# The rows' two parts kept in the order of the features, and twelve gather products moved ahead of the branch

## The chip, the cores and the metric

One core of a Trainium2 chip runs the whole program. The metric is device time in microseconds, from the start to the end of one execution. The kernel before took 949.39 us (median of three runs, 949.18 to 949.49). All profile rows are of one further execution, which took 949.4 us and whose span in the trace is 947.4 us. Engines: PE is TensorE with PEld its weight loads, DVE is VectorE, ACT is ScalarE, POOL is GpSimd, SP issues most transfers.

## The reference

Two transformer blocks in float32 over 256 tokens of 1024 features. The change touches only the mixture of experts at the end of the second block:

```python
xn = rms_norm(h, ffn_norm_g)                      # (1, 256, 1024)
group_prob = softmax(xn @ w_rg + b_rg)            # 4 groups, the best one is taken
sel = expert logits of that group                 # 8 experts, the best two are taken
out = zeros_like(xn)
for e in range(32):
    hid = silu(xn @ w_gate[e]) * (xn @ w_up[e])   # 1024 -> 256
    out = out + (hid * cw[..., e:e + 1]) @ w_down[e]
h = h + out                                       # then the final rms_norm
```

## The kernel before

The program first runs all dense layers (up to about 700 us), in which every float32 product is made of three products of rounded parts (`pe_mm3`, L493 to L495). The experts follow in one of two forms, and a branch on a number in memory (`flag`, read at L2970, tested at L2977) chooses between them: when no expert has more than `CAP` = 48 tokens, the sparse form runs, else the dense form. These inputs take the sparse form.

In the sparse form the tokens of each expert are gathered by products. `SEL0` is a 0/1 matrix: for 128 tokens and for each of a set of `SET_E` = 8 experts it has 48 columns, one for each slot of the expert. The normalised rows are the stationary operand (128 tokens by 128 features), the 384 columns of `SEL0` are the moving one, and what comes out in PSUM is 128 features by 8 x 48 slots. As rounding would lose bits, the rows are kept in two parts, `XN[0]` (high, rounded, called XNH in the profile) and `XN[1]` (low, the rest, XNL), and both go through the same product. There are four sets of experts (q = 0 to 3), 8 chunks of features (k), 2 parts and 2 tiles of tokens (t): 32 products for each set, 128 in all. All are made at L2481 (`pe_gather`), except for the first twelve of set 0 (high part, k = 0 to 5, both tiles), which are made at L2569 at the start of `pe_sparse`.

Chunk k holds the features k, k + 8, k + 16 and so on, since the weights of the experts are loaded in that order. In the kernel before, the rows are put into that order when the parts are made. `by_chunks` is a view of X with chunks ahead of features: ScalarE reads X by it with a step of 8 elements (32 bytes) and writes `XN4[0]` without gaps (L1532, two instructions of 1024 elements); VectorE does the same for the low part (`low`, L2013, eight instructions of 256 elements). Each stationary operand `XN4[i][:, t, k]` is then 128 neighbouring elements.

The order around the branch is written out by hand, engine by engine:

- PE: the router's products, 9 warm-up products, three products that count ranks (L1002 to L1005, semaphore `rank_mm`), 2 warm-up products (`pe_warm`, L996; each is two instructions), the branch, the twelve products of L2569, then twenty of L2481: low part of k = 0 to 3, high part of k = 6 and 7 (their banks come free by ScalarE's evictions), low part of k = 4 to 7. Then `pe_rise` (L2507), the first expert pair.
- DVE: routing, then the largest count (`most`, L2017), the ranks (L2019), a copy of the count to an integer (`flag`, L2021), the two halves of `SEL0` (`dve_mark`, L1944, semaphore `sel`), eight low parts in the order k = 0 and 1 of both tiles, k = 2 and 3, and so on (semaphore `xn_lo`), then the combine weights.
- ACT: the high parts (L1532), two small exponentials, the branch, then the evictions of the gathered features (`act_gather`, L2623).

All five engines wait for `flag` and read it before they branch.

Of the kernel before, what the change touches and what calls it, by code (L numbers as in the profile page):

```python
# [7 lines left out]
ALU = mybir.AluOpType  # L8
ACT = mybir.ActivationFunctionType
# [155 lines left out]
def build(nc, A, out):  # L165
    with ExitStack() as ctx:
# [202 lines left out]


        ROUTER = U["router", 0, 0]

        def raw_of(i):
            kc, w = shape_of(i)
# [379 lines left out]
        def pe_main():  # L754
# [238 lines left out]
            def pe_warm(n):  # L993

                for _ in range(n):
                    PE.matmul(PB[0][:, 0:256], ident, cst("upper", 256), start=True, stop=True, skip_group_check=True)  # L996
# [7 lines left out]
                      skip_group_check=True)  # L1004
            PE.matmul(PB[1][:, 64:96], UO[:, 128:256], MK[:, 32:64], start=False, stop=True, skip_group_check=True).then_inc(S["rank_mm"], 1)  # L1005
            pe_warm(2)

# [163 lines left out]
        def act_main():  # L1173
# [355 lines left out]
                ACTE.activation(UO[:, 128 * i:128 * i + 128], cst("upper", 128, 128 * i), ACT.Copy).then_inc(S["const_r"], 1)  # L1529
            ACTE.wait_ge(*scaled("ffn"))  # L1530
            for t in range(2):
                ACTE.activation(XN4[0][:, t], by_chunks[:, t], ACT.Copy, scale=rs_of["ffn"][:, t:t + 1]).then_inc(S["xn_hi"], 1)  # L1532
            ACTE.wait_ge(S["route_e"], 1)
            ACTE.activation(eg, eg, ACT.Exp).then_inc(S["step_a"], 1)
            ACTE.wait_ge(S["route_e"], 2)
# [18 lines left out]
        def dve_then(ins):  # L1554

            steps[0] += 1
            ins.then_inc(S["step_d"], 1)

        def dve_after():
            DVE.wait_ge(S["step_d"], steps[0])  # L1560
# [356 lines left out]
        def rt(n):  # L1917
            o = rt_at[0]
            rt_at[0] += n
            return KW[:, o:o + n]  # L1920
# [4 lines left out]
        fst, snd, q_e = [v3(rt(8), 2, 4) for _ in range(3)]  # L1925
        e2 = rt(2)
        rank, cw = rt(64), rt(64)
        most, flag = rt(1), rt(1).bitcast(I32)
        wa, wb = rt(2), rt(2)

        def b3(ap, n):
# [16 lines left out]
        def dve_route():  # L1948
            L3 = v3(L, 2, 36)
            DVE.wait_ge(S["logits"], 2)  # L1950
            DVE.wait_ge(*scaled("ffn"))
            b1 = banks_of(("router", 0))[1]
            for t in range(2):
                DVE.scalar_tensor_tensor(L3[:, t], PB[b1][:, 36 * t:36 * t + 36], rs_of["ffn"][:, t:t + 1], rb, ALU.mult,
                                         ALU.add).then_inc(evicted(("router", 0))[0], 1)
            DVE.wait_ge(*evicted(("router", 0)))
            G, E = L3[:, :, 0:4], L3[:, :, 4:36].rearrange("p t (g n) -> p t g n", g=4)
            order8 = cst("order", 8, 4).unsqueeze(1).unsqueeze(1).to_broadcast([128, 2, 4, 8])

            def step(ins):  # L1960

                dve_then(ins)
                return steps[0]

            def behind(n):
                DVE.wait_ge(S["step_d"], n)

            a = step(DVE.tensor_reduce(fst, E, AXX, ALU.max))
            g = step(DVE.tensor_reduce(gm, G, AXX, ALU.max))
            behind(a)  # L1970
            a = step(DVE.tensor_tensor(v_e, E, b8(fst), ALU.is_equal))
            behind(g)
            for t in range(2):
                g = step(DVE.scalar_tensor_tensor(v_a[:, t], G[:, t], gm[:, t:t + 1], cst("order", 4), ALU.is_equal, ALU.mult))
            behind(a)
            a = step(DVE.tensor_tensor(v_e, v_e, order8, ALU.mult))
            behind(g)
            g = step(DVE.tensor_reduce(q_a, v_a, AXX, ALU.max))
            DVE.tensor_tensor(eg, G, b3(gm, 4), ALU.subtract).then_inc(S["route_e"], 1)
            behind(a)  # L1980
            a = step(DVE.tensor_reduce(q_e, v_e, AXX, ALU.max))
            behind(g)
            g = step(DVE.tensor_tensor(og, v_a, b3(q_a, 4), ALU.is_equal))
            behind(a)
            a = step(DVE.tensor_tensor(o1, v_e, b8(q_e), ALU.is_equal))
            behind(a)
            a = step(DVE.scalar_tensor_tensor(el, o1, NEG, E, ALU.mult, ALU.add))
            behind(a)
            a = step(DVE.tensor_reduce(snd, el, AXX, ALU.max))
            behind(a)  # L1990
            a = step(DVE.tensor_tensor(v_e, el, b8(snd), ALU.is_equal))
            behind(a)
            a = step(DVE.tensor_tensor(v_e, v_e, order8, ALU.mult))
            behind(a)
            a = step(DVE.tensor_reduce(q_e, v_e, AXX, ALU.max))
            behind(a)
            a = step(DVE.tensor_tensor(o2, v_e, b8(q_e), ALU.is_equal))
            behind(a)
            a = step(DVE.tensor_tensor(el, o1, o2, ALU.add))
            behind(a)  # L2000
            DVE.tensor_tensor(MK[:, :].rearrange("p (t g n) -> p t g n", t=2, g=4), el, b8(og), ALU.mult).then_inc(S["mask_d"], 1)

            a = step(DVE.tensor_tensor(snd, snd, fst, ALU.subtract))
            behind(a)
            a = step(DVE.tensor_tensor(snd, snd, og, ALU.mult))
            behind(a)
            DVE.tensor_reduce(e2, snd, AXX, ALU.add).then_inc(S["route_e"], 1)

            def low(t, r):

                DVE.wait_ge(S["xn_hi"], t + 1)
                hi, lo = [x[:, t, 2 * r:2 * r + 2] for x in XN4]
                DVE.scalar_tensor_tensor(lo, by_chunks[:, t, 2 * r:2 * r + 2], rs_of["ffn"][:, t:t + 1], hi.bitcast(F), ALU.mult,  # L2013
                                         ALU.subtract).then_inc(S["xn_lo"], 1)

            DVE.wait_ge(S["rank_mm"], 1)
            dve_then(DVE.tensor_reduce(most, PB[1][:, 64:96], AXX, ALU.max))  # L2017
            DVE.wait_ge(S["mask_d"], 1)
            DVE.scalar_tensor_tensor(rank, PB[1][:, 0:64], 1.0, MK[:, :].bitcast(F), ALU.add, ALU.mult).then_inc(S["rank"], 1)  # L2019
            dve_after()  # L2020
            DVE.tensor_copy(flag, most).then_inc(S["flag"], 1)  # L2021
            DVE.wait_ge(S["rank"], 1)
            for t in range(2):
                dve_mark(SEL0, t, 0).then_inc(S["sel"], 1)
            for r in range(4):
                for t in range(2):
                    low(t, r)
            DVE.wait_ge(S["step_a"], 1)
            dve_then(DVE.tensor_reduce(pg, eg, AXX, ALU.add))
            DVE.wait_ge(S["step_a"], 2)  # L2030
            dve_then(DVE.tensor_scalar(wa, e2, 1.0, None, ALU.add))
            dve_after()
            dve_then(DVE.reciprocal(pg, pg))
            dve_then(DVE.reciprocal(wa, wa))
            dve_after()
            dve_then(DVE.scalar_tensor_tensor(wa, wa, 0.5, pg, ALU.mult, ALU.mult))
            dve_after()
            dve_then(DVE.tensor_tensor(wb, wa, e2, ALU.mult))
            one, two = [o.rearrange("p t g n -> p t (g n)") for o in (o1, o2)]
            dve_then(DVE.tensor_tensor(one, one, b3(wa, 32), ALU.mult))  # L2040
            dve_after()
            dve_then(DVE.tensor_tensor(two, two, b3(wb, 32), ALU.mult))
            dve_after()
            dve_then(DVE.tensor_tensor(o1, o1, o2, ALU.add))
            dve_after()
            DVE.tensor_tensor(cw[:, :].rearrange("p (t g n) -> p t g n", t=2, g=4), o1, b8(og), ALU.mult).then_inc(S["weights"], 1)
# [363 lines left out]
        def sparse(late):  # L2410
# [16 lines left out]
                return p // PS + 1 if p % PS == PS - 1 and p + 1 < NP else 0  # L2427

            def gather_bank(q, k):
                return PB[(6, 7, 2, 3, 0, 1, 6, 7)[k] if q == 0 else (6, 7, 4 + (PS * q - 1) % 2)[k % 3]]  # L2430

            def rise_bank(p):
                return PB[4 + p % 2]
# [7 lines left out]
            def selected(q, t=1):  # L2441
                return S["sel"], 2 * q + t + 1
# [21 lines left out]
            def pe_gather(q, k, parts=(0, 1)):  # L2464
# [4 lines left out]
                elif q > 0 and k == 0:  # L2469
                    PE.wait_ge(*selected(q))  # L2470
                if q == 0 and 1 in parts:
                    PE.wait_ge(S["xn_lo"], 2 + 2 * (k // 2))
                if q > 0 and k < 2:
                    PE.wait_ge(S["yy_lo"], 2 * (PS * q - 3) + k + 1)
                elif q > 0 and k == 2:
# [84 lines left out]
                        m.then_inc(S["spread"], 1)  # L2560

            def pe_sparse():
                PE.wait_ge(S["evict1"], K_LAST[1])
                PE.wait_ge(S["evict0"], K_LAST[0])
                for t in range(2):
                    PE.wait_ge(*selected(0, t))
                    PE.wait_ge(S["xn_hi"], t + 1)
                    for k in range(6):
                        PE.matmul(gather_bank(0, k)[:, 0:384].rearrange("p (e n) -> p e n", e=SET_E), XN4[0][:, t, k], slots_of(SEL0, t),  # L2569
                                  start=(t == 0), stop=False, skip_group_check=True)  # L2570
                for k in range(4):
                    pe_gather(0, k, (1,))
                for k in (6, 7):
# [384 lines left out]
        normed = ExitStack()  # L2958
        XN = [sbe("XNH", 2048, R, normed), sbe("XNL", 2048, R, normed)]
        SEL0, MK, UO = [sbe(n, w, R, normed) for n, w in (("SEL0", 1024), ("MK", 64), ("UO", 256))]  # L2960
        XN4 = [x[:, :].rearrange("p (t k q) -> p t k q", t=2, k=8) for x in XN]
        by_chunks = X[:, :].rearrange("p (t q k) -> p t k q", t=2, k=8)
        sp_main()
        pe_main()
        act_main()
# [32 lines left out]
```

## Time and profile before

| | |
|---|---|
| median of three runs | 949.39 us |
| the profiled execution | 949.4 us, of which the span is 947.4 us |
| PE busy | 936.2 us, 99% of the span |
| DVE busy, ACT busy | 533.4 us, 471.5 us |
| granted TensorE clock over the span | 0.996 |
| gather products (L2569, L2481) | 12 + 116 recorded |
| first product of the gather | 710.04 us |
| first product of the first expert pair | 716.08 us |

Read it so: the engine busy times say who has no idle time; the chain of waits, followed back from the last instruction, says which engine held the end at each moment; the timeline of the few microseconds around the branch says who waits for whom there. "PEld" rows are the loads of the stationary operand, one for each product, which run beside the product before. The time between the starts of two loads in a row is their spacing; it is found from a merged row as (length of the row minus one load) divided by (count minus one).

### The profile page before, as it was taken

To read this page: it belongs to the slowest core of one execution; us is meant where nothing else is said; L and a number is where in the kernel's file an instruction comes from. 1 tells how busy PE (TensorE), PEld (TensorE's weight loads), DVE (VectorE), ACT (ScalarE), POOL (GpSimd) and SP (SyncE) were. 2 spreads that over 40 slices of the span, in tenths; PEclk is the share of its full clock that TensorE was granted. 3 is DMA by queue.
4 is the path that set the end of the run, shared out by engine and by line. 5 is a ranking of instruction groups with operands and counts; after the bars stand their busy time and mean duration, and the time that the engine had idled before them with its cause. 6 is when DMAs were issued, how large, how long until landed. Compare 5 with 4: busy or idle time off the path is not lost.

```text
span 947.4 us, 14062 instructions
## 1 busy us (share of the span) xinstructions
PE 936.2 (99%) x5793; PEld 763.5 (81%) x5793; DVE 533.4 (56%) x835; ACT 471.5 (50%) x728; POOL 4.2 (0%) x13
## 2 busy tenths in 40 slices
PE   9999999999999999999999999999999999999996
PEld 8989887888889999999889888889876665666553
DVE  5888996775766555655676875676353212122213
ACT  5488856857454544444566756445452121313113
POOL 1000000000000000000000000000000000000000
PEclk9999999999999999999999999999999999999998
DMA  9944565535565555554655735476758999999992
GB/s 321 304 147 158 198 222 178 162 106 178 178 190 188 178 178 178 180 191 154 202 150 181 235 121 178 134 265 224 272 203 301 409 409 409 409 408 409 409 409 112
DMA packets 89861, 223.55 MB, mean 236 GB/s; under 512 B 9161, under 2 KB 14018, under 8 KB 89794
## 3 DMA queue, kind: packets, MB, share of 16 engines
q1 hardware_dynamic: 87488, 219.62, 64.7%
q10 hardware_dynamic: 2306, 2.99, 0.9%
q8 instruction: 48, 0.79, 0.4%
q14 instruction: 19, 0.16, 0.1%
HBM read 221.54 MB, written 1.05 MB: 235 GB/s over the span
## 4 chain that ended last, share of the span: by engine, by line
PE 98%; DVE 1%; ACT 0%; issue 0%; POOL 0%; POOLq 0%
PE pb L493 22%; PE pb L495 21%; PE pb L494 21%; PE pb L2507 12%; PE pb L2530 6%; PE pb L2547 3%; PE pb L2481 2%; PE pb L583 2%; PE pb L663 1%; PE pb L651 1%; PE pb L750 1%; PE pb L634 1%; PE pb L601 1%; PE pb L727 1%; PE pb L557 1%; PE pb L758 1%
## 5 line engine op out<-in xcount | busy, mean ns | idle before, releaser
L1566 DVE TENSOR_TENSOR wl<-raw,wh 128x2048 fp32r<-128x2048 f32 (+3 forms) x112 | 246.2, 2207 | 96.7 <-ACT wh L1016 96.4
L1016 ACT ACTIVATE wh<-raw 128x2048 fp32r<-128x2048 f32 (+3 forms) x112 | 206.7, 1852 | 109.8 <-PE pb L495 100.5
L493 PE MATMUL pb<-wh,th 128*128 128x512 f32 (+2 forms) x620 | 245.8, 396 | 0.0
L495 PE MATMUL pb<-wh,tl 128*128 128x512 f32 (+2 forms) x620 | 238.9, 385 | 0.0
L494 PE MATMUL pb<-wl,th 128*128 128x512 f32 (+2 forms) x620 | 238.6, 385 | 0.0
L493 PE MATMUL pb<-th,wh 128*128 128x256 f32 x528 | 152.7, 289 | 0.0
L494 PE MATMUL pb<-tl,wh 128*128 128x256 f32 x528 | 149.3, 283 | 0.0
L495 PE MATMUL pb<-th,wl 128*128 128x256 f32 x528 | 149.3, 283 | 0.0
L495 PEld LDWEIGHTS pb<-wh,tl 128*128 128x128 f32 x620 | 116.4, 188 | 23.4
L493 PEld LDWEIGHTS pb<-wh,th 128*128 128x128 f32 x620 | 116.5, 188 | 22.9 <-issue 2.2
L494 PEld LDWEIGHTS pb<-wl,th 128*128 128x128 f32 x620 | 116.7, 188 | 20.6
L493 PEld LDWEIGHTS pb<-th,wh 128*128 128x128 f32 x528 | 101.1, 191 | 2.7 <-issue 1.5
L494 PEld LDWEIGHTS pb<-tl,wh 128*128 128x128 f32 x528 | 101.2, 192 | 0.5
L495 PEld LDWEIGHTS pb<-th,wl 128*128 128x128 f32 x528 | 101.1, 191 | 0.0
L2714 DVE SCALAR_TENSOR_TENSOR HS<-HS,pb 128x256 f32<-128x256 f32 x16 | 6.7, 421 | 91.3 <-ACT HS L2639 91.2
L2639 ACT ACTIVATE HS<-pb 128x256 f32<-128x256 f32 x16 | 6.1, 384 | 95.2 <-PE pb L2507 95.2
L2723 DVE TENSOR_TENSOR YL<-pb,YH 128x512 fp32r<-128x512 f32 x32 | 22.1, 692 | 36.7 <-ACT YH L2649 36.7
L2649 ACT ACTIVATE YH<-pb 128x512 fp32r<-128x512 f32 x32 | 19.1, 597 | 41.1 <-PE pb L2530 41.1
L1032 ACT ACTIVATE th<-pb,PC 128x256 fp32r<-128x256 f32 x45 | 18.8, 480 | 25.7 <-PE pb L583 25.7
L2705 DVE TENSOR_REDUCE CS<-pb 64x1 f32<-64x2 f32 x32 | 5.0, 157 | 45.2 <-ACT SET L2616 44.6
L2507 PE MATMUL pb<-raw,XG 128*64 128x256 f32 x256 | 30.4, 379 | 0.0
L2507 PEld LDWEIGHTS pb<-raw,XG 128*64 128x64 f32 x256 | 18.3, 137 | 10.3 <-issue 1.5
(424 smaller groups left out, 1123.9 us busy)
## 6 DMA issues: line engine op xcount, KB each, us to landing
raw<-in_w_in SPq DMA_DIRECT2D x31, 1024.0 KB, 5.5
raw<-in_w_up SPq DMA_DIRECT2D x16, 1024.0 KB, 5.6
raw<-in_w_down SPq DMA_DIRECT2D x16, 1024.0 KB, 5.0
raw<-in_w_exp_gate SPq DMA_DIRECT2D x9, 1024.0 KB, 18.2
raw<-in_w_xkv SPq DMA_DIRECT2D x8, 1024.0 KB, 5.1
raw<-in_w_exp_down SPq DMA_DIRECT2D x8, 1024.0 KB, 17.3
raw<-in_w_exp_up SPq DMA_DIRECT2D x7, 1024.0 KB, 14.8
my<-in_w_exp_down SPq DMA_DIRECT2D x7, 1024.0 KB, 16.2
```

Source lines behind the costliest of these rows:

```text
L493: PE.matmul(o, lh, rh, start=start, stop=False, skip_group_check=True)
L494: PE.matmul(o, lh, rl, start=False, stop=False, skip_group_check=True)
L495: return PE.matmul(o, ll, rh, start=False, stop=stop, skip_group_check=True)
L583: m = PE.transpose(PB[b][:, 128 * t:128 * t + 128], x, ident)
L1016: ACTE.activation(hi_of(i), raw_of(i), ACT.Copy).then_inc(S["hi"], 1)
L1566: DVE.tensor_tensor(lo_of(i), raw_of(i), hi_of(i).bitcast(F), ALU.subtract).then_inc(S["lo"], 1)
L2481: m = PE.matmul(b[:, 0:384].rearrange("p (e n) -> p e n", e=SET_E), XN4[i][:, t, k], slots_of(SEL0, t), start=(t == 0 and i == 0), stop=(t ...
L2507: m = PE.matmul(b[64 * j:64 * j + 64, 256 * g:256 * g + 256], XG[:, c + CAP * j:c + CAP * j + 64], w[:, j, k], start=(r == 0 and k == 0), ...
L2530: m = PE.matmul(down_bank(p, h)[64 * j:64 * j + 64, :], HT[p % 2][:, 128 * k + 64 * j:128 * k + 64 * j + 64], w[:, j, 512 * h:512 * h + 51 ...
L2547: m = PE.matmul(PB[2 * t + h][:, :], SET[p % 4][:, 128 * t:128 * t + 128], YY[p % 2][i][:, 512 * h:512 * h + 512], start=(p == 0 and i == ...
L2649: ACTE.activation(YY[p % 2][0][:, 512 * h:512 * h + 512], down_bank(p, h)[:, :], ACT.Copy).then_inc(S["yy_hi"], 1)
L2723: DVE.tensor_tensor(lo, down_bank(p, h)[:, :], hi.bitcast(F), ALU.subtract).then_inc(S["yy_lo"], 1)
```

## The change

The parts are written in the order in which X has the features, so that ScalarE and VectorE read and write without gaps: two instructions of 1024 elements each for the low part instead of eight of 256, and the same two for the high part. `XN4` becomes the strided view, so each of the 128 stationary operands of the gather is now read with a step of 8 elements (32 bytes). The waits for the low part become one: all of it (`xn_lo` at 2). The largest count is reduced straight into the integer `flag`, without the copy. The twelve products of L2569 move from behind the branch to behind the two last warm-up products, in front of it, with waits for `sel`, `xn_hi` and the evictions of the banks that they use.

```diff
+        FIRST_BANKS = (6, 7, 2, 3, 0, 1, 6, 7)
@@ pe_main
             pe_warm(2)
+            PE.wait_ge(*evicted(("router", 0)))
+            PE.wait_ge(*evicted(("w_xo_2", 1)))
+            for t in range(2):
+                PE.wait_ge(S["sel"], t + 1)
+                PE.wait_ge(S["xn_hi"], t + 1)
+                for k in range(6):
+                    PE.matmul(PB[FIRST_BANKS[k]][:, 0:384].rearrange("p (e n) -> p e n", e=SET_E), XN4[0][:, t, k], slots_of(SEL0, t),
+                              start=(t == 0), stop=False, skip_group_check=True)
@@ act_main
-                ACTE.activation(XN4[0][:, t], by_chunks[:, t], ACT.Copy, scale=rs_of["ffn"][:, t:t + 1]).then_inc(S["xn_hi"], 1)
+                ACTE.activation(XN2[0][:, t], Xv[:, t], ACT.Copy, scale=rs_of["ffn"][:, t:t + 1]).then_inc(S["xn_hi"], 1)
@@ dve_route
-            def low(t, r):
+            def low(t):
                 DVE.wait_ge(S["xn_hi"], t + 1)
-                hi, lo = [x[:, t, 2 * r:2 * r + 2] for x in XN4]
-                DVE.scalar_tensor_tensor(lo, by_chunks[:, t, 2 * r:2 * r + 2], rs_of["ffn"][:, t:t + 1], hi.bitcast(F), ALU.mult,
+                hi, lo = [x[:, t] for x in XN2]
+                DVE.scalar_tensor_tensor(lo, Xv[:, t], rs_of["ffn"][:, t:t + 1], hi.bitcast(F), ALU.mult,
                                          ALU.subtract).then_inc(S["xn_lo"], 1)
-            dve_then(DVE.tensor_reduce(most, PB[1][:, 64:96], AXX, ALU.max))
+            DVE.tensor_reduce(flag, PB[1][:, 64:96], AXX, ALU.max).then_inc(S["flag"], 1)
...
-            dve_after()
-            DVE.tensor_copy(flag, most).then_inc(S["flag"], 1)
...
-            for r in range(4):
-                for t in range(2):
-                    low(t, r)
+            for t in range(2):
+                low(t)
@@ pe_gather
                 if q == 0 and 1 in parts:
-                    PE.wait_ge(S["xn_lo"], 2 + 2 * (k // 2))
+                    PE.wait_ge(S["xn_lo"], 2)
@@ pe_sparse
-                PE.wait_ge(S["evict1"], K_LAST[1])
-                PE.wait_ge(S["evict0"], K_LAST[0])
-                for t in range(2):
-                    PE.wait_ge(*selected(0, t))
-                    PE.wait_ge(S["xn_hi"], t + 1)
-                    for k in range(6):
-                        PE.matmul(gather_bank(0, k)[:, 0:384].rearrange("p (e n) -> p e n", e=SET_E), XN4[0][:, t, k], slots_of(SEL0, t),
-                                  start=(t == 0), stop=False, skip_group_check=True)
@@ buffers
-        XN4 = [x[:, :].rearrange("p (t k q) -> p t k q", t=2, k=8) for x in XN]
-        by_chunks = X[:, :].rearrange("p (t q k) -> p t k q", t=2, k=8)
+        XN2 = [v3(x, 2, D) for x in XN]
+        XN4 = [x[:, :].rearrange("p (t q k) -> p t k q", t=2, k=8) for x in XN]
```

## Rows read from the trace of the kernel before

**Rows 1.** The page's parts 1 and 4: engine busy times and the chain's shares.

```profile
PE 936.2 (99%) x5793; PEld 763.5 (81%) x5793; DVE 533.4 (56%) x835; ACT 471.5 (50%) x728; POOL 4.2 (0%) x13
...
PE 98%; DVE 1%; ACT 0%; issue 0%; POOL 0%; POOLq 0%
```

**Rows 2.** Windows table, 716 to 937 us: PE, PEld, DVE, ACT, POOL busy; clock; DMA share.

```profile
716.00:937.00 221.00, 221.00 (x1563) 137.41 (x1563) 45.66 (x108) 51.88 (x109) 0.00 (x0) 1.00 0.96 380
```

**Rows 3.** Chain of waits around the branch and later gathers: start us, us, what.

```profile
709.09 0.54 DVE SEL L1944
709.63 0.41 issue
710.04 2.35 PE pb L2569 x12
712.40 3.75 PE pb L2481 x20
...
757.59 5.66 PE pb L2481 x32
...
869.33 5.65 PE pb L2481 x32
```

**Rows 4.** Timeline around the branch: start us, us, engine line operation [idle before <-releaser].

```profile
705.20 4.19 ACT L1532 ACTIVATE XNH<-X,SM 128x1024 fp32r<-128x1024 f32 x2
...
708.52 1.11 PE L996 MATMUL pb<-CT 128*128 128x256 f32 x4
...
708.95 0.14 DVE L2021 CAST KW<-KW 128x1 int32<-128x1 f32 x1
709.06 1.02 DVE L1944 TENSOR_TENSOR SEL<-CT,KW 128x384 fp32r<-128x384 f32 x2
...
710.01 5.12 DVE L2013 SCALAR_TENSOR_TENSOR XNL<-X,SM,XNH 128x256 fp32r<-128x256 f32 x8
710.01 2.06 PEld L2569 LDWEIGHTS pb<-SEL,XNH 128*128 128x128 f32 x12 [0.79 <-issue]
...
712.06 1.42 PEld L2481 LDWEIGHTS pb<-SEL,XNL 128*128 128x128 f32 x8
...
712.85 3.64 ACT L2623 ACTIVATE XG<-pb,SM 128x384 f32<-128x384 f32 x7 [2.49 <-PE pb L2481]
...
715.18 0.65 PEld L2481 LDWEIGHTS pb<-SEL,XNL 128*128 128x128 f32 x4 [0.23 <-DVE XNL L2013]
...
716.08 0.20 PEld L2507 LDWEIGHTS pb<-mth,XG 128*64 128x64 f32 x4 [0.25 <-issue]
```

**Rows 5.** Groups by form, VectorE and ScalarE: busy us, mean ns.

```profile
L2013 DVE SCALAR_TENSOR_TENSOR XNL<-X,SM,XNH 128x256 fp32r<-128x256 f32 x8 | 5.1, 707 | 0.0
...
L2271 DVE SCALAR_TENSOR_TENSOR X<-pb,SM,X 128x512 f32<-128x512 f32 x4 | 2.8, 746 | 1.7 <-PE pb L495 1.7
...
L2288 DVE SCALAR_TENSOR_TENSOR X<-GA,X 128x512 f32<-128x512 f32 x4 | 2.8, 692 | 0.1
...
L1777 DVE TENSOR_TENSOR RC<-RC,SM 128x1024 f32<-128x1024 f32 x2 | 2.4, 1218 | 0.0
...
L1016 ACT ACTIVATE wh<-raw 128x1024 fp32r<-128x1024 f32 x4 | 4.3, 1065 | 9.2 <-PE pb L495 9.2
```

**Rows 6.** Weight loads by line: duration ns min/median/max, first and last start.

```profile
L768 PEld LDWEIGHTS pb<-CT,X x16: 185/193/207, 6.5 to 8.4; 128*128 128x128 f32 x16
...
L2515 PEld LDWEIGHTS pb<-CT,HS x32: 137/140/144, 726.1 to 923.6; 128*128 128x128 f32 x32
...
L2481 PEld LDWEIGHTS pb<-SEL,XNL x64: 186/188/189, 712.1 to 874.5; 128*128 128x128 f32 x64
```

**Rows 7.** Timeline of first load pairs: strided turned, contiguous turned, contiguous plain.

```profile
7.60 0.30 PEld L768 LDWEIGHTS pb<-CT,X 128*128 128x128 f32 x2
...
923.37 0.20 PEld L2515 LDWEIGHTS pb<-CT,HS 128*128 128x128 f32 x2 [0.81 <-issue]
...
703.87 0.30 PEld L996 LDWEIGHTS pb<-CT 128*128 128x128 f32 x2
```

More of the change, by code:

```diff
@@ L1927, in build @@
         rank, cw = rt(64), rt(64)
-        most, flag = rt(1), rt(1).bitcast(I32)
+        flag = rt(1).bitcast(I32)
         wa, wb = rt(2), rt(2)
@@ L2429, in gather_bank @@
             def gather_bank(q, k):
-                return PB[(6, 7, 2, 3, 0, 1, 6, 7)[k] if q == 0 else (6, 7, 4 + (PS * q - 1) % 2)[k % 3]]
+                return PB[FIRST_BANKS[k] if q == 0 else (6, 7, 4 + (PS * q - 1) % 2)[k % 3]]
             def rise_bank(p):
```

## The prediction

> **What bounds the kernel now.** I read the page first: PE is busy 99% of the span and holds 98% of the chain [rows 1]. Then I asked for the stretch behind the gather: from 716 to 937 us PE is busy in all 221.00 us, at a granted clock of 1.00 [rows 2]. So whatever moves the start of the first expert pair (716.08 us) moves the end of the kernel by as much, and whatever makes a product slower is paid in full; nothing on VectorE or ScalarE is worth anything unless PE waits for it. The chain of waits gives the one place where PE does wait near the change: VectorE's first half of SEL ends at 709.63, then come 0.41 us of "issue", which is the branch, then the twelve products (2.35 us) and the twenty (3.75 us) [rows 3]. The timeline shows PE out of work from 709.63 (its warm-up row, 708.52 + 1.11) to 710.01, and one more stop: the load at 715.18, which waited for the last low part [rows 4]. In the other three sets a gather costs 5.65 to 5.66 us for 32 products, 0.177 us each, one set behind the other without a gap; the first and the last of three rows are shown [rows 3].
>
> **The edits off PE's path.** The high parts take 4.19 us strided, two instructions of 2.1 us [rows 4]; a copy of 1024 elements without gaps takes 1.065 us [rows 5]. They would be done at 705.20 + 2 x 1.07 = 707.3 instead of 709.4. The first consumer, the first product, also needs SEL, which is there at 709.63: the 2.1 us saved on ScalarE are worth nothing. The integer copy of the count (0.14 us at 708.95) goes, so the flag comes some 0.2 us sooner. The marks (709.06) wait for the ranks, not for the copy, and stay where they are. SP's last transfer behind the branch is the final gain, needed at the end, so an earlier branch gives it nothing either.
>
> **The twelve products in front of the branch.** They can start when SEL's first half is there: 709.63 plus the 0.05 us that another wait took from VectorE's end (710.01 + 5.12 = 715.13) to PE's load (715.18) [rows 4], so 709.68 at best and 710.04, as before, at worst. The spacing of loads is (1.42 - 0.19) / 7 = 0.176 us [rows 4]. Twelve take 2.1 us and end the row at 711.8 to 712.2. The branch costs PE at most 709.09 to 710.04, 0.95 us, and now lies beside these products. Looked at alone this edit gains up to 0.36 us. It gains only if what comes next is ready.
>
> **What is late next: the low parts.** The marks end as before, and the first low part starts at 710.01 [rows 4]. Before, the pair for k = 0 and 1 was ready after two of eight strided instructions of 0.707 us [rows 5], about 711.3, long before PE came to it at 712.06; PE met the low parts only at the very end. Now PE needs both instructions of 1024 elements. A two-operand instruction of 1024 elements without gaps takes 1.218 us, and the per-partition scalar adds 0.746 - 0.692 = 0.054 us [rows 5]: 1.27 us each. Eight instructions in a row overlapped by (8 x 0.707 - 5.12) / 7 = 0.08 us each, so the two end at 710.01 + 2.54 - 0.08 = 712.47, and the first load of a low part comes at 712.52. VectorE saves 5.12 - 2.46 = 2.66 us, and yet its product is the thing PE waits for, since the first piece comes 1.2 us later than before.
>
> **The twenty products.** After a stop the second load follows by 0.11 us, and each further one by 0.176: the last starts at 712.52 + 0.11 + 18 x 0.176 = 715.80. Before, it started at 715.18 + 0.65 - 0.19 = 715.64 [rows 4]. On the way, the high products of k = 6 and 7 need the first and the second eviction. Evictions started 0.79 us behind the first low load (712.85 against 712.06) and follow at 3.64 / 7 = 0.52 us [rows 4], so the second ends near 712.52 + 0.79 + 1.04 = 714.35; PE comes to k = 6 at 712.52 + 0.11 + 7 x 0.176 = 713.86, and to k = 7 at 714.21. That is a wait of 0.14, and the loads behind it close up by 0.176 - 0.11: I take 0.1. The first expert pair thus starts 0.26 us later than before, near 716.34.
>
> Bounds of this stretch: with no wait for the low parts at all, 32 loads from 709.68 give the last at 709.68 + 0.11 + 30 x 0.176 = 715.07, a gain of 0.57 us. At the other end, if the long instruction goes by twice the 512-element one with its scalar, 2 x 0.746 = 1.49 us, the low parts end at 712.91, 0.44 us later still, a loss of 0.70 us. I take +0.26 because the 1024-element row is the nearest in size.
>
> **The stride of 128 weight loads.** This is the only term that could be large. The gather's loads take 0.188 us each [rows 6]; what counts is how closely they can follow each other, for the product needs 0.176. The trace has no plain load with a stride, but it has the turning products of the first layer, which read X with the same step of 8. Their loads take 0.193 us where loads of turning products without a stride take 0.140 [rows 6]: the stride shows. The first two loads of a series go without waiting for a product, and give the spacing: strided turned 0.30 - 0.19 = 0.11 us, unstrided turned 0.20 - 0.14 = 0.06, plain unstrided 0.30 - 0.19 = 0.11 [rows 7]. So a strided read delivers 128 columns in 0.11 us, and a plain load takes no more than that in any case. I take 0 for the stride: the load stays far under 0.176. Bounds: it can't fall below 0, as the product sets the pace. Adding the turned loads' 0.05 us gives a spacing of 0.16, still 0. Doubling it (ScalarE's strided read doubled too, 2.1 against 1.065) gives 0.22, 0.044 us over the product's pace.
>
> A rule of the Trainium skill speaks against the change (Advanced Engine Details and Errata, SBUF Cachelines): a line has 16 bytes, and an access pattern that goes to another line each time pays a penalty. A step of 32 bytes does so each time. By it every load would pay, and the kernel would come out as in the first rival below. Another page (TensorE: Matmul & The Clock Gate, LDWEIGHTS) gives a load's time by its columns alone, columns / 1.2 ns, an estimate of 107 ns for 128, with no word of a stride; by it nothing is paid. The trace bears out a penalty on turned loads, which starts from 0.06, and lands at the 0.11 which a plain load has anyway.
>
> **The sum.** 0 (ScalarE) + 0 (flag) + 0.26 (gather of set 0) + 0 (stride) on the profiled execution's 949.4 gives 949.7 us; that execution stands 0.01 us from the median of the runs. For this kernel 0.2% is 1.9 us, about what a measurement can tell from no change; the forecast is no change. Its own range is 949.4 - 0.57 to 949.4 + 0.70, or 948.8 to 950.1. Chance 0.68.
>
> **Rivals.**
>
> 1. Slower: the plain load reads its stationary operand in two passes, and each pays the strided 0.11 us, so that the spacing is 0.22. For it: a plain load takes twice as long a spacing as a turned one of the same 128 columns, 0.11 against 0.06, as two passes would. Against it: the slower pace may as well be that of the array, with each element read once. It decides where a load's spacing passes 0.176. Price: 0.044 x 96 products of sets 1 to 3 and x 20 of set 0 = 5.1 us; the first twelve take 12 x 0.22 = 2.6 and end at 712.3, under the wait for the low parts. Time 949.7 + 5.1 = 954.8. At its cheapest, with the longest strided load (0.207 [rows 6]) taken off the pair, a pass is 0.30 - 0.207 = 0.093 us and two are 0.186: 0.010 x 116 = 1.2 us, 950.9. Chance 0.16.
> 2. PE does its branch only when the twelve products have left its queue: 711.8 + 0.95 = 712.75 instead of 712.52, so 949.9. Against it: before, the branch went on beside the warm-up products, which ran until 709.63. Chance 0.10.
> 3. The low parts are quicker than their nearest rows and PE never waits for them: 948.8. Only an instruction of 1024 elements in about 0.7 us would do that; none of VectorE's two-operand rows is like it. Chance 0.06.
>
> **How the numbers follow.** All but the first rival lie within 1.9 us of 949.4. Of the first, nine tenths or so lie beyond it: slower 0.15. A gain over 1.9 us has no place to come from, as PE waits only some 0.6 us in all around the change; 0.02 is left for what no row shows. Same is the rest, 0.83. The range runs from 948.8 to 951.2: it holds the forecast and the two small rivals whole and the cheap end of the first.
>
> **What would show it.** In the changed kernel: the high parts in about 2.1 us together; two low parts of 1.2 to 1.3 us that end near 712.5; the twelve products from about 709.7 and a stop of PE of some 0.4 to 0.6 us behind them, ended by VectorE's XNL; the first product of the first pair at 716.1 to 716.5; and in the three later sets 5.65 us for 32 products still. The prediction is wrong if these gathers take over 6 us each, or if the loads' mean, now 0.188, rises by 0.1 us or more; or if PE's stop behind the twelve isn't there.

## The result: 8.4 us slower, all of it in the 128 strided products

| | before | after |
|---|---|---|
| median | 949.18 us (948.9 to 949.49) | 957.57 us (957.4 to 958.02) |
| ratio | | 1.0088 [1.0077, 1.0098] |
| span of the profiled execution | 947.4 us | 956.1 us |
| granted clock over the span | 0.996 | 0.998 |

The forecast was 949.7 us, no change, with a range of 948.8 to 951.2; the median after lies 6.4 us above its upper end. The page of the kernel after, parts 1 and 4, answers to [rows 1]:

```profile
PE 945.0 (99%) x5793; PEld 773.0 (81%) x5793; DVE 530.7 (56%) x828; ACT 469.6 (49%) x728; POOL 4.2 (0%) x13
...
PE 98%; DVE 1%; ACT 0%; issue 0%; POOL 0%; POOLq 0%
```

PE is as full as before, with as many instructions, and 8.8 us busier. No wait was added: the same number of products takes longer. The chain of waits of after (start us, us, what), beside [rows 3], says which:

```profile
709.26 0.57 DVE SEL L1953
709.83 0.24 issue
710.07 3.22 PE pb L1014 x12
713.29 4.86 PE pb L2487 x20
...
759.60 7.84 PE pb L2487 x32
...
816.72 7.84 PE pb L2487 x32
...
875.72 7.84 PE pb L2487 x32
```

A later set's gather takes 7.84 us where it took 5.65: 0.245 us for a product instead of 0.177. Three sets give 3 x 2.19 = 6.57 us. In set 0 the twelve go from 2.35 to 3.22 and the twenty from 3.75 to 4.86, 1.98 us together. The twelve now begin 0.17 us sooner, counted from VectorE's last instruction ahead of the marks (MK, at 707.82 before and 708.01 after), and that MK itself came 0.19 us later in this execution. 6.57 + 1.98 - 0.17 + 0.19 = 8.57 of the 8.7 us between the spans.

The load row of L2487 (ns min/median/max, first and last start), beside [rows 6]:

```profile
L2487 PEld LDWEIGHTS pb<-SEL,XNL x64: 336/341/347, 712.9 to 883.0; 128*128 128x128 f32 x64
```

A load takes 0.341 us where it took 0.188. The timeline around the branch, which answers to [rows 4]:

```profile
705.40 2.18 ACT L1541 ACTIVATE XNH<-X,SM 128x1024 fp32r<-128x1024 f32 x2
...
708.01 0.23 DVE L2010 TENSOR_TENSOR MK<-KW 128x64 fp32r<-128x64 f32 x1
...
710.04 2.99 PEld L1014 LDWEIGHTS pb<-SEL,XNH 128*128 128x128 f32 x12 [0.62 <-issue]
...
710.20 2.47 DVE L2022 SCALAR_TENSOR_TENSOR XNL<-X,SM,XNH 128x1024 fp32r<-128x1024 f32 x2
...
712.93 2.04 PEld L2487 LDWEIGHTS pb<-SEL,XNL 128*128 128x128 f32 x8
...
718.08 0.84 PEld L2513 LDWEIGHTS pb<-mth,XG 128*64 128x64 f32 x10 [0.18 <-issue]
```

The savings off PE are there as forecast: 2.18 us on ScalarE, 2.47 on VectorE. PE has no stop behind the twelve: the low parts end at 712.67, and PE, slower now, comes to them only at 712.93.

### The profile page after: what moved, and what is told of

Its sections match the earlier page's. It is cut to its first block, busy times and chain, and to the rows that moved or that the text cites. A ratio compares the mean times of both kernels' runs of the same rounds, so it can differ in the third digit from the quotient of the medians.

```text
span 956.1 us, 14055 instructions
## 1 busy us (share of the span) xinstructions
PE 945.0 (99%) x5793; PEld 773.0 (81%) x5793; DVE 530.7 (56%) x828; ACT 469.6 (49%) x728; POOL 4.2 (0%) x13
## 3 DMA queue, kind: packets, MB, share of 16 engines
q10 hardware_dynamic: 2306, 2.99, 0.9%
## 4 chain that ended last, share of the span: by engine, by line
PE 98%; DVE 1%; ACT 0%; issue 0%; POOL 0%; POOLq 0%
PE pb L494 21%; PE pb L496 21%; PE pb L495 21%; PE pb L2513 12%; PE pb L2536 6%; PE pb L2487 3%; PE pb L2553 3%; PE pb L584 2%; PE pb L664 1%; PE pb L652 1%; PE pb L751 1%; PE pb L635 1%; PE pb L728 1%; PE pb L602 1%; PE pb L558 1%; PE pb L759 1%
```

## The experiments

Except in the three kernels that only measure loads, "first pair" is the time from the MK row to the first load of the first expert pair: 8.26 us before, 10.07 after.

**1. The stride alone** (four runs). One line of the kernel before; everything else, the branch and the strided engines too, stays as it was:

```diff
-        XN4 = [x[:, :].rearrange("p (t k q) -> p t k q", t=2, k=8) for x in XN]
+        XN4 = [x[:, :].rearrange("p (t q k) -> p t k q", t=2, k=8) for x in XN]
```

> The kernel before with one line changed: the parts are kept in the order of X and the stationary operand is read with a step of 8; the twelve products stay behind the branch, and the eight low pieces and the copy of the count stay. (Each low piece now covers other features than its wait is for, so the low part may be read early by a product: the features are mixed up, which leaves the work the same.) Theory S (all of the 8.4 us is the stride, 128 products at 0.067 us more): 949.4 + 128 x 0.067 = 958.0 us, 7.84 us for 32 products in each of the three later sets. Rival M (a good part comes from the moved products and the later low part): the later sets take 7.84, but the total stays clearly under, at most 956.5.

Where this text says that features are mixed up, it was mistaken: the low pieces are written through the same view, so each chunk is the same as in the kernel before, only laid out with gaps. The time is read as that of the whole computation.

Measured: 957.94 us (957.66 to 958.24), beside 949.29 us of the kernel before on the same chip, ratio 1.0089 [1.0073, 1.0104], as much as the whole change. The chain of this kernel:

```profile
710.27 3.23 PE pb L2569 x12
713.50 4.86 PE pb L2481 x20
...
759.80 7.84 PE pb L2481 x32
```

3.23, 4.86 and 7.84 us, the values of the changed kernel to 0.01. The stationary operand's step is enough for the whole loss. The rest of the change is worth 0.17 us where it acts (the first pair comes at 10.24 us here and at 10.07 in the changed kernel) and nothing that the total can show.

**2. Steps 1 and 2.** The changed kernel with its moved products and short `flag`, but with b chunks side by side, so that the stationary operand has a step of b elements. The low parts come in eight pieces again, in the order in which PE needs them, with the waits of the kernel before. With b = 1 the rows lie as they did before; with b = 2 a step is 8 bytes:

```diff
+        XNP = [x[:, :].rearrange("p (t a q b) -> p t a q b", t=2, a=4, b=2) for x in XN]
+        XP = X[:, :].rearrange("p (t q a b) -> p t a q b", t=2, a=4, b=2)
+        def chunk_of(i, t, k):
+            return XNP[i][:, t, k // 2, :, k % 2]
...
-                ACTE.activation(XN2[0][:, t], Xv[:, t], ACT.Copy, scale=rs_of["ffn"][:, t:t + 1]).then_inc(S["xn_hi"], 1)
+                ACTE.activation(XNP[0][:, t], XP[:, t], ACT.Copy, scale=rs_of["ffn"][:, t:t + 1]).then_inc(S["xn_hi"], 1)
```

> The changed kernel with the stride alone undone: the rows' parts lie in the order of the chunks again (ScalarE and VectorE read X with a step of 8, eight low pieces), the twelve products stay in front of the branch and the count is reduced straight to an integer. Theory S: sets 1 to 3 take 5.65 us for 32 products again, and the total is that of the kernel before within 0.3 us, 949.0 to 949.5, since the last low piece (near 715.2) still sets the end of the first gather. Rival M: 2 us or more of the loss stay, 951 or more. A gain over 0.6 us would say that the front place is worth more than I think.

> As the changed kernel, but neighbouring chunks lie in pairs: the stationary operand has a step of 2 elements (8 bytes), ScalarE and VectorE read X in pairs of neighbours, eight low pieces of 256. Theory A (lines of 16 bytes, two hits in each): no penalty on the loads, 5.65 us for 32 products, and as the low pieces may be quicker than 0.707 us when they read pairs, 948.7 to 949.4 us. Theory B (any step costs): 32 products take between 5.65 and 7.84 us, some 6.5, and the total is 951 to 954.

Measured in eleven runs each, beside the same 949.29 us: step 1 949.28 us, ratio 0.9998 [0.9989, 1.0007]; step 2 949.24, 0.9999 [0.9990, 1.0008]. The gathers are back at 5.66. The profiled execution of step 1 took 951.08 us and was 1.7 us late already before this place (MK at 709.50, where the kernel before has 707.82), so places are counted from MK. First the timeline of step 1, with the last low loads:

```profile
709.50 0.22 DVE L2010 TENSOR_TENSOR MK<-KW 128x64 fp32r<-128x64 f32 x1
...
711.69 5.13 DVE L2022 SCALAR_TENSOR_TENSOR XNL<-X,SM,XNH 128x256 fp32r<-128x256 f32 x8
...
716.87 0.65 PEld L2488 LDWEIGHTS pb<-SEL,XNL 128*128 128x128 f32 x4 [0.40 <-DVE XNL L2022]
...
717.77 1.49 PEld L2514 LDWEIGHTS pb<-mth,XG 128*64 128x64 f32 x16 [0.25 <-issue]
```

Then the timeline of step 2:

```profile
705.65 2.33 ACT L1541 ACTIVATE XNH<-X,SM 128x1024 fp32r<-128x1024 f32 x2
...
708.27 0.23 DVE L2010 TENSOR_TENSOR MK<-KW 128x64 fp32r<-128x64 f32 x1
...
710.46 3.26 DVE L2022 SCALAR_TENSOR_TENSOR XNL<-X,SM,XNH 128x256 fp32r<-128x256 f32 x8
...
716.14 1.49 PEld L2514 LDWEIGHTS pb<-mth,XG 128*64 128x64 f32 x16 [0.24 <-issue]
```

And its chain:

```profile
710.33 2.33 PE pb L1014 x12
712.66 3.56 PE pb L2488 x20
...
757.67 5.66 PE pb L2488 x32
```

With step 1 the twelve start 0.16 us sooner, and all of it is given back: PE waits 0.40 us for the last strided low part [0.23 in rows 4], and the first pair comes at 8.27 us. Pairs take that wait away: VectorE's eight pieces take 3.26 us instead of 5.13, the twenty run in 3.56 instead of 3.75, and the first pair comes at 7.88, 0.38 us sooner than before. That is the earliest first pair of all versions, but 0.38 of 949 us is too little to show in the interval of the total.

**3. Step 4** (four runs), the same kernel with b = 4 (16 bytes) and the low parts in four pieces.

> As the changed kernel, but chunks lie in fours: the stationary operand has a step of 4 elements (16 bytes, one element in each line), four low pieces of 512. Line theory: the full penalty, as at step 8, 0.233 us for each product by the first series, 7.5 us for 32 products, total 949.2 + 128 x 0.057 = 956.5 us. Rival (the cost grows with the distance): about half of the way from step 2 to step 8, 6.7 us for 32, total near 953.

Measured: 956.99 us beside 949.04, ratio 1.0086 [1.0070, 1.0103]. Its chain:

```profile
874.72 7.66 PE pb L2488 x32
```

Of the 2.19 us that step 8 adds to a gather, step 4 adds 2.01 and step 2 nothing. The loss doesn't grow with the distance; nearly all of it is there once each element lies in another 16 bytes.

**4. Loads by themselves** (three kernels, one run each; none computes anything of the reference). Long products fill PE, then come 32 products, with only the step and the moving columns changed:

```python
for i in range(32): PE.matmul(PB[i % 4][0:128, 0:32], SR[:, 0:509:4], MR[:, 0:32], ...)   # L202
...
for i in range(32): PE.matmul(PB[i % 4][0:128, 0:384], SR[:, 0:509:4], MR[:, 0:384], ...) # L214
```

> This kernel computes nothing of the reference: it holds only series of 32 products each, with the stationary operand read at steps of 1, 2, 3, 4, 8 and 16 elements, as rounded float32 (32, 384 and 512 moving columns), bfloat16, plain float32 and turned float32, and at the end a product for the output. It measures the disputed load by itself. Theory A (lines of 16 bytes): a load pays as soon as a step leaves fewer than two elements in a line. For float32 the steps 1 and 2 space their loads by 0.108 us, steps 4, 8 and 16 by 0.216 us, all three alike; step 3 lies between. With 384 moving columns 0.176 for steps 1 and 2, 0.243 for 4, 8, 16. Theory B (the cost grows with the distance): 1, 2, 4, 8, 16 give five rising spacings, and 16 is clearly over 0.216. Theory C (two reads for each column of a float32 load): bfloat16 loads without a step are spaced by half the float32 ones, 0.055 us, and by about 0.108 with a step of 16 bytes or more, that is, the same penalty for one read. Rival to C (the array takes a column in two cycles whatever the type): bfloat16 unstrided is 0.108 too and a step costs it nothing.

Measured, us for each product at 384 moving columns: step 1 0.176 (the middle value, as its first half ran at half the clock), step 2 0.173, step 3 0.178, step 4 0.233, step 8 0.243, step 16 0.225. At 512 moving columns: step 1 0.227, step 8 0.244. All three steps from 4 on lie close together, as theory A has it and theory B has not, though at 0.225 to 0.243 and not at one value. The series with 32 moving columns and steps from 2 on ran in a stretch at half the clock, which gave a second answer. The loads (ns min/median/max, first and last start) at step 4 with 32 columns and with 384:

```profile
L202 PEld LDWEIGHTS pb<-movr,statr x32: 329/330/332, 45.3 to 52.6; 128*128 128x128 f32 x32
...
L214 PEld LDWEIGHTS pb<-movr,statr x32: 308/330/330, 86.2 to 93.4; 128*128 128x128 f32 x32
```

And the windows of the two (PE, PEld, DVE, ACT, POOL busy, granted clock, DMA):

```profile
45.30:52.60 7.30, 7.30 (x33) 7.30 (x33) 0.00 (x0) 0.00 (x0) 0.00 (x0) 0.50 0.00 0
86.20:93.40 7.20, 7.20 (x33) 7.20 (x32) 0.00 (x0) 0.00 (x0) 0.00 (x0) 1.00 0.00 0
```

One load takes 0.330 us at a granted clock of 0.50 (1.2 GHz) and at 1.00 (2.4 GHz), and 32 of them start within 7.3 and 7.2 us, 0.233 us apart both times. What paces this load is not TensorE's clock. A load without the penalty does follow it. Here is step 2 in the same half-clock stretch (busy us, mean ns):

```profile
L198 PEld LDWEIGHTS pb<-movr,statr 128*128 128x128 f32 x32 | 6.9, 331 | 0.0
```

These follow each other at 0.213 us, and at 0.126 at a clock of 1.00 (next kernel). So going from step 2 to step 4 costs 0.020 us at half the clock and 0.107 at full clock.

The second kernel takes series of 16 with few moving columns, behind 24 long products each, to keep the clock up and let the load alone set the pace. The granted clock was 1.00 over most of the series, and 0.97, 0.94 and 0.86 over those with steps 16, 4 and 12, whose last loads ran at half the clock; their spacing stayed the same through the fall (0.267 us before and after it at step 12).

> This kernel, too, computes nothing of the reference: series of 16 products, each behind 24 long products (512 moving columns) that keep the granted clock up, which had fallen in the short series of the first one. Line theory (a step that leaves fewer than two float32 elements in 16 bytes pays, whatever the further distance): with 128 moving columns steps 1 and 2 are spaced by 0.11 us, 4, 5, 6, 7, 8, 12 and 16 by 0.22 to 0.245, step 3 (12 bytes) by under 0.18; a start one element on changes nothing. Rival (distance or bank of the memory): 5, 6 and 7 or 12 and 16 fall outside that band. Per-column theory: 96 columns at step 8 take three quarters of 0.24, 64 columns half, 0.12. Two-reads theory: turned float32 loads, one read for each column, take 0.057 at step 1 and half of the plain strided time, 0.11 to 0.12, at 8 and 16; bfloat16 at 96 columns, where the fast way of loading may be off, takes as the turned ones if it reads once.

Its timeline of PEld (start, length of 16). Plain fp32r loads of 128 columns with step 16, 4, 1, 8, 2, 3 and 12; 96 columns with step 1 and 8; turned loads with step 8 and 1; bf16 of 128 columns with step 1 and 8; moving operands of 256 columns with step 1 and 2 (stationary step 1):

```profile
31.72 3.61 PEld L197 LDWEIGHTS pb<-movr,statr 128*128 128x128 f32 x16
...
42.03 3.82 PEld L200 LDWEIGHTS pb<-movr,statr 128*128 128x128 f32 x16
...
52.41 1.98 PEld L203 LDWEIGHTS pb<-movr,statr 128*128 128x128 f32 x16
...
59.70 3.92 PEld L206 LDWEIGHTS pb<-movr,statr 128*128 128x128 f32 x16
...
68.89 2.08 PEld L209 LDWEIGHTS pb<-movr,statr 128*128 128x128 f32 x16
...
76.24 2.92 PEld L212 LDWEIGHTS pb<-movr,statr 128*128 128x128 f32 x16
...
93.39 4.34 PEld L218 LDWEIGHTS pb<-movr,statr 128*128 128x128 f32 x16
...
161.22 1.58 PEld L239 LDWEIGHTS pb<-movr,statr 128*96 128x96 f32 x16
...
168.09 3.02 PEld L242 LDWEIGHTS pb<-movr,statr 128*96 128x96 f32 x16
...
190.22 1.98 PEld L251 LDWEIGHTS pb<-CT,statf 128*128 128x128 f32 x16
...
197.49 1.90 PEld L254 LDWEIGHTS pb<-CT,statf 128*128 128x128 f32 x16
...
227.03 0.47 PEld L266 LDWEIGHTS pb<-movb,statb 128*128 128x128 bf16 x16 [0.26 <-issue]
...
233.03 1.08 PEld L269 LDWEIGHTS pb<-movb,statb 128*128 128x128 bf16 x16 [0.26 <-issue]
...
270.36 2.09 PEld L284 LDWEIGHTS pb<-movr,statr 128*128 128x128 f32 x16
...
277.74 3.64 PEld L287 LDWEIGHTS pb<-movr,statr 128*128 128x128 f32 x16
```

One plain load of 128 columns takes 0.192 us at step 1, 0.196 at 2, 0.261 at 3, 0.329 at 4, 0.337 at 8, 0.313 at 16 and 0.369 at 12. By (length of the row minus one load) / 15 the spacings are 0.119, 0.126, 0.177, 0.233, 0.239, 0.220 and 0.265 us. At step 3 three of four elements open a new 16 bytes, at step 4 and over each does: 0.177 / 96 and 0.233 / 128 are both 1.8 ns, and 96 columns at step 8 take (3.02 - 0.28) / 15 = 0.183, or 1.9 ns each. So the spacing of these fp32r loads fits the longer of 0.93 ns for each column and about 1.8 ns for each new 16 bytes. (Each mean holds the first gap, which still waits for the long product ahead: at step 1 it is 0.226 us and the other fourteen are 0.112, at step 2 they are 0.118. That puts the load without a stride at 0.87 ns for each column and changes the rest by little.) Two things don't fit: step 12, and the order 16 below 4 below 8 (1.72 to 1.87 ns). No experiment explains them. Steps 5, 6 and 7 take 0.224 to 0.231 us, and a start one element further on changes nothing (0.125 at step 2, 0.239 at step 8), so, step 12 apart, neither the distance nor the place where the operand begins decides.

Turned loads follow each other at 0.12 us with step 8 and with step 1 alike, though the first unstrided pair of [rows 7] was only 0.06 apart; so their products seem to set the pace here. A strided turned load thus needs at most 0.12 us, where a strided plain one of the same 128 columns needs 0.24.

The third kernel asks what the price goes by, elements or bytes, on bf16.

> Again nothing of the reference, series of 16 products behind long ones. What is open: why a plain strided load of float32 takes twice a turned one. Two-reads theory is already against the series before (bfloat16 at 96 columns and a step of 8, 16 bytes, took 0.176 us, float32 0.180). Access theory: each column of a plain load is one access, which takes some 1.8 us per thousand when its line was not the last one's, whatever the type. Then bfloat16 at 96 columns takes 0.045 to 0.09 us at steps 1, 2 and 4 (2 to 8 bytes) and 0.18 at 8 and 16; and one element read again and again (step 0) costs no more than step 1, 0.11. Moving operands: float32 at step 2 already took 0.228 for 256 columns; if their pace is set by lines too, step 3 is as slow and step 1 in 8 pieces of 48 columns costs a few ns over one piece of 384.

Its timeline, bf16 of 96 columns with step 1, 4 (8 bytes) and 8 (16 bytes):

```profile
32.10 1.13 PEld L197 LDWEIGHTS pb<-movb,statb 128*96 128x96 bf16 x16
...
44.93 1.65 PEld L203 LDWEIGHTS pb<-movb,statb 128*96 128x96 bf16 x16
...
51.86 2.95 PEld L206 LDWEIGHTS pb<-movb,statb 128*96 128x96 bf16 x16
```

With one load at 0.123, 0.186 and 0.273 us the spacings are 0.067, 0.098 and 0.179 us. bf16 with 16 bytes of step costs what fp32r does (0.183) at half the bytes, though without a stride it is the quicker one (0.067 against 0.094); and half the new places cost a little over half. One fp32r element read again and again takes what step 1 does (0.119), as expected. For these two kinds of plain load, fp32r and bf16 of 96 columns, the price goes by the 16-byte places and not by elements or their size. It isn't one price for every load: bf16 of 128 columns pays a quarter of it (last section).

The Trainium skill has this rule (Advanced Engine Details and Errata, SBUF Cachelines: an access that goes to another 16-byte line each time pays a penalty). Every plain load here with 16 bytes of step or more agrees in that it pays, and the page gives no price. The other rule of the Trainium skill (TensorE: Matmul & The Clock Gate, LDWEIGHTS: columns over 1.2, an estimate of 107 ns for 128) lies near the 119 ns measured at step 1, and from step 4 on the measured spacing is twice that.

**5. What a product then costs: the longer of two, or a sum?** (four runs each). All 128 products with 512 moving columns instead of 384: each expert's 16 empty slots are taken in, PE also waits until they are zeroed, and ScalarE's eviction leaves them out again. The first kernel has step 1 and eight low pieces, the second step 8 and the two long ones. The product's line in the second:

```diff
-                        m = PE.matmul(b[:, 0:384].rearrange("p (e n) -> p e n", e=SET_E), XN4[i][:, t, k], slots_of(SEL0, t), ...
+                        m = PE.matmul(b[:, 0:512], XN4[i][:, t, k], SEL0[:, 512 * t:512 * t + 512], ...
```

> The changed kernel without the stride, and with each gather product over 512 moving columns, the 16 empty slots of each expert included, instead of 384 (the eviction leaves them out again). 32 products take 32 x 0.227 = 7.3 us; total 949.3 + 128 x 0.051 = 955.8 us. It is the counterpart of the next one.

> The changed kernel (step 8) with 512 moving columns. Theory P (a product's pace is the longer of its own 0.227 and the strided load's 0.243): 7.8 us for 32 products, total 128 x 0.016 = 2 us over its counterpart without the stride, 957.8 us, hardly more than the changed kernel itself. Theory Q (the strided load adds its 0.067 us to every product, whatever its length): 32 products take 9.4 us, total about 964 us.

Measured, beside 949.04 us before: step 1 956.02 us, ratio 1.0074 [1.0058, 1.0091]; step 8 958.91 us (957.75 to 959.97), ratio 1.0104 [1.0088, 1.0121]. The chain of step 1:

```profile
874.11 7.28 PE pb L2489 x32
```

The chain of step 8:

```profile
875.99 7.93 PE pb L2488 x32
```

0.228 and 0.248 us for a product. With longer products the same stride costs 2.9 us instead of 8.6, since the products cover nearly all of the load. A sum of the two (9.4 us for 32) is out. The pace is the longer of product (0.228) and load (0.244 at 512 moving columns in experiment 4), to 0.004 us.

**6. The low parts late, without the stride** (one run). In the changed kernel the stride hid one step of the forecast, the stop behind the twelve. Here the step-2 kernel makes PE wait for six of the eight low pieces before the first low product:

```diff
-                    PE.wait_ge(S["xn_lo"], 2 + 2 * (k * 4 // 8))
+                    PE.wait_ge(S["xn_lo"], max(6, 2 + 2 * (k * 4 // 8)))
```

> The kernel with the step of 2, but PE waits for six of the eight low pieces before the first low product, 6 x 0.41 = 2.45 us behind the first piece's start, which is where the two long instructions of the changed kernel end (2.47 us). It shows the term of my forecast by itself, which the slow loads hid in the changed kernel: that PE stops behind the twelve products. By the forecast the last of the twelve starts at about +2.1 us from the first, PE then stands for 0.4 to 0.6 us, and the first expert pair starts 0.5 to 0.7 us later than with the step of 2 (7.88 us behind VectorE's MK, so 8.4 to 8.6; the kernel before had 8.26). Rival: the wait costs nothing, 7.9, since the evictions or the branch end later anyway.

Measured: 950.39 us, a single time, in which an early transfer far ahead of this place came late too, so I read the place itself. Timeline:

```profile
708.56 0.23 DVE L2010 TENSOR_TENSOR MK<-KW 128x64 fp32r<-128x64 f32 x1
...
713.27 1.37 PEld L2488 LDWEIGHTS pb<-SEL,XNL 128*128 128x128 f32 x8 [0.62 <-DVE XNL L2022]
...
717.05 0.41 PEld L2514 LDWEIGHTS pb<-mth,XG 128*64 128x64 f32 x6 [0.24 <-issue]
```

The stop is there, 0.62 us, ended by VectorE. The low load comes 4.71 us behind MK, where the forecast had 712.52 - 707.82 = 4.70. The first pair comes at 8.49 us, 0.61 later than with step 2 (0.5 to 0.7 expected) and 0.23 later than in the kernel before, where the forecast had 0.26.

## Why the prediction was wrong

- **ScalarE's save worth nothing, the flag nothing: right for ScalarE.** The first product comes 2.06 us behind MK with ScalarE's strided high parts (step 1) and with the quicker ones (step 2) alike. The flag was not tried by itself; what it gave is somewhere in the 0.17 us of the next point.
- **The twelve in front of the branch, up to 0.36 us: right in kind.** They start 0.16 to 0.17 us sooner: the first load comes 0.21 us behind SEL's first half (710.04 against 709.26 + 0.57), where the best case had 0.05. The branch lies beside them: the twelve loads end at 710.04 + 2.99 = 713.03, and the next load starts at 712.93, one spacing behind the last of the twelve. Rival 2, PE's branch behind the products, is out.
- **The low parts late next, +0.26 us: right without the stride, void with it.** VectorE's two instructions took 2.47 us (2.46 forecast). But twelve products at 0.245 us instead of 0.176 end after the low parts, so the stop vanished in the changed kernel. Experiment 6 shows it without the stride, 0.23 us.
- **Rival 3, low parts in time, 948.8: out.** Nothing was quicker than its row.
- **The stride of 128 loads, 0: this is the step that failed.** The text put it so: "a strided read delivers 128 columns in 0.11 us, and a plain load takes no more than that in any case". The 0.11 was the spacing of turned loads, which need at most half of what plain ones do with the same step (0.12 against 0.24 in one kernel). It was taken as a limit of reading, valid for both kinds. The row showed that the stride costs something, 0.06 to 0.11 us in spacing, a factor of 1.8. The argument that a plain load has that time anyway was an argument about one mechanism; nothing in the trace bore it out. In its place the runs showed a spacing of 0.239 us for strided plain loads by themselves and 0.245 us for each product in the gathers. The same factor on the plain load's own 0.11 would have given 0.20, 0.026 us over the product's 0.176; the loads by themselves show a factor of 2.0, 0.239 against 0.119.
- **The bound was too low as well.** The upper end of 0.22 doubled a rounded spacing of 0.11. Measured is 0.243 to 0.245, and as only the part over 0.176 counts, 0.02 us of spacing are a third of the price: 0.067 x 128 = 8.6 us against 0.044 x 116 = 5.1.
- **Rival 1 had the place and the direction; its mechanism stays open.** The load does decide where its spacing passes the product's 0.176 us, and experiment 5 shows the same with a longer product. Its two passes are neither shown nor excluded. Against them: if fp32r took two and the quicker bf16 one, bf16 of 96 columns would pay half of fp32r's price at 16 bytes of step, and it pays as much. But both may read twice, and a strided plain load does take twice the 0.12 us that bounds a turned one. What the runs do give is the count of 16-byte places. The rival also let the first twelve go free under the wait for the low parts. Nearly so: PE reached the low parts 4.92 us behind MK, 0.22 later than the forecast wait would have let it go on.
- **The signs.** All three that the prediction named against itself came: gathers over 6 us (7.84), loads longer by 0.1 us or more (0.188 to 0.341), and no stop behind the twelve.

## What to carry to other kernels

Let the stationary operand of a product have a step of at most 8 bytes, by keeping neighbours in pairs: PE's plain fp32r loads (0.126 against 0.119 us), ScalarE (2.33 us, against 2.18 without gaps and 4.19 strided) and VectorE (0.49 us for a piece of 256 elements, against 0.707 strided) all read pairs at or near full pace. From 16 bytes of step on, a plain fp32r load of 128 columns takes 0.22 to 0.27 us. What that costs is the part by which it passes the product itself: 0.067 us at 384 moving columns, 0.02 at 512, both at a granted clock of 1.00. Price an operation only from a row of its own kind; where the only row is of another kind and shows that an effect exists, put that factor on the near side's own number before it is called hidden, and ask first of each save (here 2.0 + 2.7 us on ScalarE and VectorE) whether anything waits for it.

## What the runs showed of the hardware that I had not expected

- A strided plain load's pace is the same at a granted clock of 0.50 and of 1.00 (0.233 us at step 4), while at step 2 it goes from 0.213 to 0.126 us. At half the clock the stride is nearly free.
- bf16 loads of 128 columns are quicker than either expectation of the first load kernel (0.055 or 0.108 without a stride): they go from (0.47 - 0.10) / 15 = 0.025 us to (1.08 - 0.18) / 15 = 0.060 at step 8, a quarter of fp32r's price for as many new places; with 96 columns bf16 pays 0.179. The quick loads of bf16 are quick at strides too, so the 1.8 ns for each new place holds for fp32r and for bf16 of 96 columns only.
- The moving operand has a price of its own, and sooner: 256 fp32r moving columns take (2.09 - 0.19) / 15 = 0.127 us at step 1 and (3.64 - 0.21) / 15 = 0.229 at step 2, where the stationary operand pays next to nothing. Why it is sooner, and whether it goes by 16-byte places, no run tells.
